# The opening of a joining stage in a two-block layer: row loads, weight pieces, router tables and the first tile's mixture in another order

## The reference, cut to what matters

```python
mixed = (jax.nn.sigmoid(g_rwkv) * (o_rwkv @ w_branch_rwkv[l])
         + jax.nn.sigmoid(g_diff) * (o_diff @ w_branch_diff[l]))
x = x + mixed @ w_out[l]
h = rms_norm(x, norm_ffn[l])
# the first lines of the router, which the same stage also computes:
(hf @ w_group) + b_group            # 4 columns
(hf @ w_er) + b_er                  # 32 columns
```

## Time and profile before

| what | us |
|---|---|
| median of 3 runs | 3413.39 (3413.06 to 3414.01) |
| the profiled execution, its own time | 3413.98 |
| its span, first to last instruction | 3412.1 |
| mean granted TensorE clock, as a share of full speed | 0.913 |
| the joining stage in the span, about | 1077 to 1356 |

### The profile page before, as it was taken

One profiled execution on the slowest core, in us unless ns is written; L12 is line 12 of the kernel. 1 busy time (PEld: TensorE's weight loads), 2 busy tenths in 40 slices (PEclk: granted clock), 3 DMA queues, 4 the chain that ended last, 5 costly groups with the idle time before them and its releaser, 6 DMA issues. The chain is left out here.

```text
span 3412.1 us, 53150 instructions
## 1 busy us (share of the span) xinstructions
PE 2944.2 (86%) x21240; PEld 2520.9 (74%) x21240; DVE 1911.7 (56%) x2344; ACT 1275.3 (37%) x1812; POOL 711.1 (21%) x448
## 2 busy tenths in 40 slices
PE   8999988887675797699999959799999895968699
PEld 7999976777343686588877847699999774745487
DVE  3365735775484433788888846400178675665421
ACT  3000004553553331577777734201111265532311
POOL 3222303332270000112222100133223141210000
PEclk9999997998687898799999979899999896978899
DMA  5465321010413532899999953333566703041421
GB/s 182 163 208 181 135 91 60 31 34 12 82 67 124 198 121 98 297 399 399 399 398 399 397 187 115 134 134 126 171 201 210 264 36 144 7 143 36 180 99 49
DMA packets 255884, 572.37 MB, mean 168 GB/s; under 512 B 25232, under 2 KB 99184, under 8 KB 254112
## 3 DMA queue, kind: packets, MB, share of 16 engines
q1 hardware_dynamic: 207744, 456.54, 37.3%
q10 hardware_dynamic: 37936, 74.40, 5.9%
q0 software_dynamic: 10032, 39.07, 3.5%
HBM read 442.35 MB, written 126.42 MB: 167 GB/s over the span
## 5 line engine op out<-in xcount | busy, mean ns | idle before, releaser
L386 PE MATMUL pin_psum<-pin_sb_w,pin_sb_hT 128*128 128x354 f32 (+1 forms) x5376 | 977.0, 344 | 15.5 <-DVE pin_sb_hT L332 5.7
L386 PEld LDWEIGHTS pin_psum<-pin_sb_w,pin_sb_hT 128*128 128x128 f32 x5376 | 937.5, 189 | 52.5 <-DVE pin_sb_hT L332 6.4
L4248 DVE TENSOR_TENSOR moe_sb_wlo<-moe_sb_raw,moe_sb_whi 128x2048 fp32r<-128x2048 f32 x192 | 437.7, 2286 | 93.2 <-ACT moe_sb_whi L4060 93.1
L4060 ACT ACTIVATE moe_sb_whi<-moe_sb_raw 128x2048 fp32r<-128x2048 f32 x192 | 367.3, 1916 | 138.9 <-DMA moe_sb_raw<-in_w_gate 48.4
L309 ACT ACTIVATE pin_sb_xt<-pin_psum,pin_sb_ss 128x353 f32<-128x353 f32 (+1 forms) x112 | 63.7, 589 | 565.2 <-PE pin_psum L386 495.6
L361 DVE TENSOR_SCALAR pin_sb_xt<-pin_psum,pin_sb_ss 128x353 f32<-128x353 f32 (+1 forms) x112 | 69.0, 624 | 330.7 <-PE pin_psum L386 330.5
L4322 PE MATMUL moe_psum<-moe_sb_whi,moe_sb_xhi 128*128 128x512 f32 x512 | 204.8, 400 | 19.5 <-DVE moe_sb_xlo L4252 19.5
L262 POOL CAST pin_sb_w<-pin_sb_raw 128x2832 fp32r<-128x2832 f32 (+1 forms) x26 | 74.5, 2865 | 629.8 <-PE pin_psum L386 585.0
L4322 PE MATMUL moe_psum<-moe_sb_whi,moe_sb_xlo 128*128 128x512 f32 x512 | 201.5, 394 | 0.0
L4322 PE MATMUL moe_psum<-moe_sb_wlo,moe_sb_xhi 128*128 128x512 f32 x512 | 201.2, 393 | 0.0
L264 POOL TENSOR_TENSOR pin_sb_w<-pin_sb_raw,pin_sb_w 128x2832 fp32r<-128x2832 f32 (+1 forms) x26 | 187.9, 7226 | 3.9 <-issue 0.7
(11 more groups left out here) (702 smaller groups left out, 5689.4 us busy)
## 6 DMA issues: line engine op xcount, KB each, us to landing
moe_sb_raw<-in_w_gate SPq DMA_DIRECT2D x64, 1024.0 KB, 12.4
moe_sb_raw<-in_w_up SPq DMA_DIRECT2D x64, 1024.0 KB, 14.0
moe_sb_raw<-in_w_down SPq DMA_DIRECT2D x64, 1024.0 KB, 12.7
scratch_proj<-pin_sb_xt ACTq DMA_DIRECT2D x16, 1412.0 KB, 6.3
scratch_proj<-pin_sb_xt ACTq DMA_DIRECT2D x12, 1792.0 KB, 6.3
pin_sb_raw<-in_w_in SPq DMA_DIRECT2D x15, 1412.0 KB, 7.1
pin_sb_raw<-in_w_in SPq DMA_DIRECT2D x11, 1792.0 KB, 8.9
scratch_ybuf<-moe_sb_yb ACTq DMA_DIRECT2D x32, 512.0 KB, 6.8
```

Of the source, the lines that this page charges most:

```text
L386: mm = te.matmul(ps[:, t, 0:cols], hT[a_part][:, k, t * P:(t + 1) * P], wt[b][w_part][:, k, :], start=(k == 0 and n == 0), stop=(k == KD - ...
L4060: s.activation(whi[q][:, :, :], raw[q][:, :, :], ACT.Copy).then_inc(hi, 1)
L4248: tt(wlo[q][:, :, :], raw[q][:, :, :], whi[q][:, :, :].bitcast(F32), ALU.subtract).then_inc(lo, 1)
```

## The change

Five edits, all inside `mix_branches`. SP loads the rows of a tile and its gates by two functions; pieces 0 to 3 are issued between the rows and the gates of tile 0, pieces 4 to 7 ahead of rows and gates of tile 1, pieces 8 to 15 ahead of x. The six router tables are issued by POOL once 8 pieces are split, ahead of its fill of `ybuf`. ACT rounds the rows of tile 1 behind `gate(0)` and ahead of piece 8. DVE does the body of tile 0 (which closes with `turn_inputs(1)`) behind piece 7 and ahead of piece 8. PE's stream is the same.

```diff
--- before.py
+++ after.py
@@ -645,9 +645,11 @@
 
         @blk.sync
         def _(sp):
-            def load_branches(t, b):
+            def load_rows(t, b):
                 sp.dma_start(ob[b][:, 0, :], o_rwkv[bass.ds(t * P, P), :]).then_inc(o_in[b], 16)
                 sp.dma_start(ob[b][:, 1, :], o_diff[bass.ds(t * P, P), :]).then_inc(o_in[b], 16)
+
+            def load_gates(t, b):
                 sp.dma_start(gt[b][:, :], proj[bass.ds(t * P, P), gcol:gcol + 2 * D]).then_inc(g_in[b], 16)
 
             def load_x(t, b):
@@ -664,32 +666,30 @@
             for b in range(2):
                 sp.sem_inc(y_st[b], 16)
                 sp.sem_inc(h_st[b], 16)
-            sp.dma_start(ident[:, :], g["ident"]).then_inc(const_in, 16)
-            load_branches(0, 0)
             def load_weights(i):
                 name, k = WEIGHTS[i]
                 if i >= NR:
                     sp.wait_ge(w_lo, i - NR + 1)
                 sp.dma_start(raw[i % NR], g[name][k * P:(k + 1) * P, :]).then_inc(w_in[i % NR], 16)
 
+            sp.dma_start(ident[:, :], g["ident"]).then_inc(const_in, 16)
+            load_rows(0, 0)
             for i in range(NR):
                 load_weights(i)
-            load_branches(1, 1)
+            load_gates(0, 0)
+            for i in range(NR, KD):
+                load_weights(i)
+            load_rows(1, 1)
+            load_gates(1, 1)
+            for i in range(KD, 2 * KD):
+                load_weights(i)
             for b in range(2):
                 load_x(b, b)
-            for dst, src in ((gain[:, :], g["norm_ffn"].partition_broadcast(P)),
-                             (wl[:, :, 0:NGRP], g["w_group"].rearrange("(k p) n -> p k n", p=P)),
-                             (wl[:, :, NGRP:], g["w_expert_router"].rearrange("(k p) n -> p k n", p=P)),
-                             (bias[:, 0:NGRP], g["b_group"].partition_broadcast(P)),
-                             (bias[:, NGRP:], g["b_expert_router"].partition_broadcast(P)),
-                             (cst[:, :], g["route_consts"])):
-                sp.dma_start(dst, src, allow_slow_non_contiguous=True).then_inc(router_in, 16)
-            for i in range(NR, 2 * KD):
-                load_weights(i)
             for t in range(NT):
                 sp.wait_ge(mturned.sem, mturned.done(t))
                 if t + 2 < NT:
-                    load_branches(t + 2, t % 2)
+                    load_rows(t + 2, t % 2)
+                    load_gates(t + 2, t % 2)
                 if t >= 1:
                     store(t - 1, (t - 1) % 2)
                 if t >= 2:
@@ -707,10 +707,19 @@
         def _(pool):
             pool.memset(zrow[:, :], 0.0)
             pool.drain()
+            pool.wait_ge(w_lo, KD)
+            for dst, src in ((gain[:, :], g["norm_ffn"].partition_broadcast(P)),
+                             (wl[:, :, 0:NGRP], g["w_group"].rearrange("(k p) n -> p k n", p=P)),
+                             (wl[:, :, NGRP:], g["w_expert_router"].rearrange("(k p) n -> p k n", p=P)),
+                             (bias[:, 0:NGRP], g["b_group"].partition_broadcast(P)),
+                             (bias[:, NGRP:], g["b_expert_router"].partition_broadcast(P)),
+                             (cst[:, :], g["route_consts"])):
+                pool.dma_start(dst, src, allow_slow_non_contiguous=True).then_inc(router_in, 16)
             pool.wait_ge(w_lo, 2 * KD)
             pool.dma_start(ybuf[NE * P:, :].rearrange("(b p) d -> p b d", p=P), over(zrow[:, :], N_BLOCKS - NE))\
                 .then_inc(fill_st, 16)
             pool.wait_ge(fill_st, 16)
+            pool.wait_ge(router_in, 96)
 
         @blk.scalar
         def _(s):
@@ -748,12 +757,12 @@
             for i in range(KD):
                 round_weights(i)
             gate(0)
+            round_inputs(1)
             for i in range(KD, 2 * KD):
                 round_weights(i)
-            for t in range(NT):
-                if t:
-                    round_mix(t - 1)
-                    gate(t)
+            for t in range(1, NT):
+                round_mix(t - 1)
+                gate(t)
                 if t >= 2:
                     norm(t - 2, t % 2)
                 if t + 1 < NT:
@@ -830,9 +839,12 @@
             for c in (copied, mixed, mcopied, added, mean, normed, hcopied, kept):
                 c.begin(ve)
             turn_inputs(0)
-            for i in range(2 * KD):
+            for i in range(KD):
                 rest_of_weights(i)
-            for t in range(NT):
+            body(0, 0, 0)
+            for i in range(KD, 2 * KD):
+                rest_of_weights(i)
+            for t in range(1, NT):
                 body(t, t % 2, t // 2)
             turn_mix(NT - 1)
             keep(NT - 3)
```

## The result

| what | before | after |
|---|---|---|
| median us | 3413.22 (3409.28 to 3414.01, 4 runs) | 3383.53 (3379.17 to 3386.58, 4 runs) |
| profiled execution, own time / span | 3413.98 / 3412.1 | 3386.58 / 3384.8 |
| mean granted TensorE clock | 0.913 | 0.919 |

The ratio is 0.9917, 95% interval 0.9902 to 0.9932: 28.3 us faster, between 23.2 and 33.4 (the two medians themselves lie 29.7 us apart). I had forecast 3391.4, 22.0 us less, with a range down to 3387.0. The direction and both waits that I named were right; the gain was larger than the range allowed.

What follows compares the result with a forecast made beforehand. PE was taken to bound the kernel, with only the joining stage's opening to shorten. Earlier pieces 11.9 plus order 10.6, less 0.5 for late pieces, gave 22.0 us less: 3391.4 from the median 3413.39, range 3387.0 to 3397.0.

Steps and rivals of the forecast that it cites:

- both waits that I named: Joining stage's opening: PE waits first for SP's late issue of piece 4, then 14.81 us for DVE's mixture.
- What bounds: Joining stage: PE sets the pace from its second tile on, so only the opening, with PE's two holes, can be shortened.
- Gates behind pieces 0 to 3: Stage opening: 1024 KB of gates no longer ahead of piece 0, which comes 2.6 us earlier, between no gain and 3.7.
- Router tables away from SP: SP's queue: piece 4 issued at 1087.5 instead of 1100.07, its rounding 11.9 us earlier, bounds 6.1 and 12.6.
- keep their distances: Pieces 5 to 7 and tile 0's branch products follow piece 4 as before, ending at 1099.1 and 1103.8.
- The clock: PE's tile 1 branches: clock can add or take about 2 us; staying up leaves 1 us of gain, counted 0.
- SP held by full queues: Rival, 0.06: full queues, not tables, held SP; tables worth 2.7 us, gain shrinks by 12.6 to 9.4, 3404.0.
- The six issues on POOL: POOL's table loads: 1.15 us per issue, landing in 20 to 27 us, hidden before `norm(0)`, cost 0.
- Mixture ahead of pieces 8 to 15: DVE's order: tile 0's mixture starts when the branch products end, bringing PE's turn of it 10.6 us forward.
- Late pieces: Pieces 8 to 15 behind the mixture: 0.5 us charged; as rival, 0.14, pieces 12 to 15 land late, 3396.1.
- The sum: Whole kernel: 22.5 us gained less 0.5 for late pieces, 22.0 us less.
- 1 us for the spread: Range's lower end: allowance for the spread of the three runs, taking 3388.1 down to 3387.0.

Runs made afterwards that it cites:

- e2: Kernel before with one edit, the gates of tile 0 loaded behind pieces 0 to 3: ratio 1.0004 to the kernel before.
- e3: Kernel before with one edit, the six router tables issued by POOL once 8 pieces are split: ratio 0.9991 to the kernel before.
- e4: Kernel before with only DVE's and ACT's new order (tile 0's body and tile 1's row rounding ahead of piece 8): ratio 0.9986 to the kernel before.
- e12: Changed kernel run again unaltered, in a later set than e1: ratio 0.9934 to the kernel before.
- e9: Kernel before run again unaltered, with its own profile: the joining stage took 277.3 us, with no long tile.
- e1: Changed kernel run again unaltered: ratio 0.9927 to the kernel before.
- e10: Changed kernel with six raw buffers for weight pieces instead of four, tile 0's gates behind piece 5: ratio 0.9933 to the kernel before.

## Why the prediction was wrong, point by point

*What bounds.* Right. Both holes shrank where they were placed: ACT's wait for piece 4 from 12.23 to 2.72 us, PE's wait for the mixture's turn from 14.81 to 4.35.

*Gates behind pieces 0 to 3.* I took 2.6 us, with bounds 0 and 3.7. Piece 0 came 3.9 us earlier in the stage, past the upper bound, which was ACT's being free: it did not wait at all. By itself the edit is worth 1.1 us at the turn (e2).

*Router tables away from SP.* **This is the term that was mis-sized.** I had piece 4 issued at 1087.5 and rounded at 1093.0, 10.5 and 16.0 us into the stage; it was 9.4 and 13.9. So 13.9 us earlier and not 11.9, also past my bound of 12.6. Two things failed in it. DVE finished piece 0 at once behind tile 0's rows, 1.1 us before I had it. And I laid the transfers end to end behind the gates at 400 GB/s, 5.5 us from piece 4's issue to its rounding, where it took 4.55, less than even the 4.84 of the earlier trace rows. Then I let pieces 5 to 7 and the products "keep their distances", and they did not: ACT waited another 1.50 us for piece 5 (0.23 before), so that by piece 7's split the lead was down to 12.6 us, and PE's clock brought it back to 13.6 at the products' end. That is 1.7 above my 11.9.

I also gave this term to the tables by name. By themselves they bring piece 4 only 6.0 us forward (e3); the rest needs the pieces ahead of rows, gates and x, an edit that the prediction never prices by itself.

*The clock.* I looked for it behind the turn and counted 0; 0.2 us came there. It paid ahead of the turn, where I had not looked: before, PE had stood idle for 8.50 us ahead of piece 4's products and did the first 6.1 us of them (1107.3 to 1113.4) at a granted clock of 0.51; after, it had no such wait, and the clock was 1.00 from 1089.3 to the products' end. From piece 7's split to that end it is 3.6 us instead of 4.6. PE before, at piece 4:

```profile
1107.28 0.79 PE L876 MATMUL mix_psum<-mix_sb_whi,mix_sb_oThi 128*128 128x512 f32 x1 [8.50 <-DVE mix_sb_wlo L781]
```

*SP held by full queues.* I gave this 0.06 and wrote it as an alternative. It is a share of the truth: one and the same table took 8.90, 6.55 and 3.44 us of SP with less and less asked for and not yet moved (by sizes asked for less GB/s times time, an estimate: 4.3, 2.8 and 2.2 MB). But the rival wanted the pieces to meet the same resistance, and in e3, with everything but the tables asked for as before, the issue of pieces 4 and 5 together took 1.61 us. Its price was also too high: it took 12.6 us from a term of 11.9.

*The six issues on POOL.* Cost 0 was right; the numbers under it were not. Issues took 0.53 to 0.92 us and not 1.15, landings 5.4 to 6.7 us and not 20 to 27. The Trainium skill's page DMA: Bandwidth & Descriptors, section Issuing engines are not separate DMA queues, has transfers of all issuing engines interleave, and e3 bears that out: with the tables on POOL's queue, pieces 11 and 12 from SP's landed late.

*Mixture ahead of pieces 8 to 15.* I took 10.6 us; it was 10.5 (from 15.85 to 5.39 us between the branch products' end and the turn). By itself 10.1.

*Late pieces.* I charged 0.5; it was 0. The chain ended at 1117.73 (`turn_mix`), 1.05 us before PE came, as worked out. That it is close is shown by e4, where 0.2 us were left, and by e12, where 0.1 were left and PE stood idle for 0.31 us ahead of its first out product.

*The sum.* In the stage 24.3 us at the first out product against 22.0: 1.7 of the pieces and 0.5 of the late pieces not paid, less 0.1 in the order, and 0.2 between the turn and the out product. The whole stage of the kernel before, without its long tile, says about 24 as well (e9). That would be 3389, inside the range. So of the 7.9 us between my 3391.4 and the measured 3383.5, 2.3 are the stage's and 5.6 lie outside it. **The second term that failed is the larger one: 1 us for the spread.** I took it from three runs within a microsecond of each other; the four executions of the changed kernel alone lie 7.4 us apart (3379.17 to 3386.58), its median came out at 3386.9 and 3388.2 in e1 and e12, and the stage begins 5 us apart in two profiles of one kernel. The later ratios of the same two kernels gave 24.9 and 22.5 us, both inside the 26.4 us to which my range reached. That the first median fell below 3387.0 is in the main bad luck, against which 1 us was no margin. (The range's own ends were worked out as 3387.1 and 3397.2 and written as 3387.0 and 3397.0.) What makes the earlier phases differ between executions I did not try, and it stays open.

## What to carry to other kernels

Count what a queue is asked for ahead of the first thing that the critical engine needs, and look in its timeline for single long issues: here one table of 1024 runs of 128 B held SP for 3.4 to 8.9 us, longer the more bytes were already asked for, and everything behind it on SP waited. Such a load belongs behind what is needed first, or on another queue. Moving loads earlier and moving the work that reads them are worth more together than apart, so judge them together, by a distance inside the stage and not by the whole time. And take the spread of a long kernel from many executions before giving a narrow range.

## What the runs showed of the hardware that was not expected

The issue of one and the same transfer (128 KB in 1024 runs) took SP 8.90, 6.55 and 3.44 us in three places, with less and less asked for ahead of it, and POOL 0.89 us. The 16 KB table just ahead of it, also in 1024 runs, took SP 0.44 to 0.95 us. The 2 KB table behind it kept SP for 3.0 to 3.8 us where the fifth table, 16 KB in as many runs, took 0.43. So neither bytes nor number of runs set the time by themselves; both long issues come right behind a table of 1024 runs. What holds them is not shown.

Transfers of POOL's queue landed in the order of their issue where a large one came first: behind 8 MB (landed 25.4 us after its issue, at 1138.5) six small tables landed 26 to 29 us after theirs, against 5.4 to 6.7 us without it.

The granted clock fell to 0.85 over a stretch in which PE was busy for 8.34 of 9 us, in a single tile of some executions (28.7 us in place of 27.05: the kernel before once of two profiles, the changed one once of three), and cost about 1.65 us each time. Behind one and the same wait of 2.46 us it fell in one execution and stayed at 1.00 in another (e10).
